# Weight sums made by DMA inside a two-layer encoder: regrouped in pairs, and started at other points

## What is computed

```python
def finish_layer(x, a, b, ga, gb, w_a, w_b, w_o, g1, b1, w_up, w_down, g2, b2):
    mix = (ga * (a @ w_a) + gb * (b @ w_b)) @ w_o
    x = layer_norm(ALPHA * x + mix, g1, b1)
    h = jnp.square(jax.nn.relu(x @ w_up)) @ w_down
    return layer_norm(ALPHA * x + h, g2, b2)
```

## Time and profile before

| what | value |
|---|---|
| three runs, median | 2154.99 us (2145.44 to 2157.51) |
| the profiled execution | 2145.24 us |
| its span, first to last instruction | 2143.4 us |
| PE busy | 2118.8 us, 99% of the span |
| DVE, ACT, POOL busy | 1471.3, 1230.3, 65.1 us |
| bytes moved by DMA | 399.27 MB, 186 GB/s in the mean |
| of them POOL's queue (q0) | 92.28 MB |

### The profile page before, as it was taken

One profiled execution on the slowest core, in us unless ns is written; L12 is line 12 of the kernel. 1 busy time (PEld: TensorE's weight loads), 2 busy tenths in 40 slices (PEclk: granted clock), 3 DMA queues, 4 the chain that ended last, 5 costly groups with the idle time before them and its releaser, 6 DMA issues.

```text
span 2143.4 us, 38213 instructions
## 1 busy us (share of the span) xinstructions
PE 2118.8 (99%) x15004; PEld 1936.0 (90%) x15004; DVE 1471.3 (69%) x2336; ACT 1230.3 (57%) x2493; POOL 65.1 (3%) x100
## 2 busy tenths in 40 slices
PE   9999999999989999999999999999999899999998
PEld 7998889999979898989889888899999798989897
DVE  6757777677869356665667577786768693566646
ACT  4457776696525356656234677766865253656561
POOL 1100000001000000000001000000010000000000
PEclk9999999999999999999999999999999999999999
DMA  7877562577894345454368765525778932454541
GB/s 256 240 279 258 210 234 82 159 238 213 222 323 104 103 130 172 151 166 139 108 189 245 289 249 202 205 88 177 223 203 255 294 105 93 139 171 152 168 148 69
DMA packets 100866, 399.27 MB, mean 186 GB/s; under 512 B 15272, under 2 KB 16936, under 8 KB 87600
## 3 DMA queue, kind: packets, MB, share of 16 engines
q1 hardware_dynamic: 67904, 191.55, 26.3%
q0 software_dynamic: 7936, 92.28, 17.2%
q10 hardware_dynamic: 24848, 112.99, 14.7%
HBM read 367.42 MB, written 118.23 MB: 227 GB/s over the span
## 4 chain that ended last, share of the span: by engine, by line
PE 96%; DMA 2%; ACT 1%; DVE 1%; issue 0%; SPq 0%; DVEq 0%; ACTq 0%
PE PS L826 9%; PE PS L828 9%; PE PS L827 9%; PE PS L1047 6%; PE PS L1049 6%; PE PS L1048 6%; PE PS L916 5%; PE PS L917 5%; PE PS L915 5%; PE PS L860 4%; PE PS L861 4%; PE PS L859 4%; PE PS L986 3%; PE PS L987 3%; PE PS L985 3%; PE PS L1175 2%
## 5 line engine op out<-in xcount | busy, mean ns | idle before, releaser
L826 PE MATMUL PS<-xt_hi,w_hi 128*128 128x320 f32 x1184 | 382.1, 323 | 0.3
L828 PE MATMUL PS<-xt_hi,w_lo 128*128 128x320 f32 x1184 | 365.7, 309 | 0.0
L827 PE MATMUL PS<-xt_lo,w_hi 128*128 128x320 f32 x1184 | 365.5, 309 | 0.0
L2539 DVE TENSOR_TENSOR w_lo<-w_raw,w_hi 128x1024 fp32r<-128x1024 f32 x146 | 177.3, 1222 | 162.0 <-ACT w_hi L1577 160.4
L2546 DVE TENSOR_TENSOR w_lo<-w_raw,w_hi 128x1024 fp32r<-128x1024 f32 (+1 forms) x176 | 199.2, 1138 | 114.9 <-ACT w_hi L1593 114.6
L1577 ACT ACTIVATE w_hi<-w_raw 128x1024 fp32r<-128x1024 f32 x146 | 153.3, 1059 | 189.6 <-PE PS L1049 155.8
L826 PEld LDWEIGHTS PS<-xt_hi,w_hi 128*128 128x128 f32 x1184 | 222.7, 188 | 5.4 <-issue 4.3
L827 PEld LDWEIGHTS PS<-xt_lo,w_hi 128*128 128x128 f32 x1184 | 223.0, 188 | 0.1
L828 PEld LDWEIGHTS PS<-xt_hi,w_lo 128*128 128x128 f32 x1184 | 222.2, 188 | 0.0
L1593 ACT ACTIVATE w_hi<-w_raw 128x1024 fp32r<-128x1024 f32 (+1 forms) x176 | 172.2, 984 | 86.1 <-PE PS L987 66.3
L1047 PE MATMUL PS<-w_hi,act_a_hi 128*128 128x512 f32 x480 | 189.7, 395 | 13.2 <-DVE rows L3005 13.2
(11 more groups left out here) (391 smaller groups left out, 5088.2 us busy)
## 6 DMA issues: line engine op xcount, KB each, us to landing
w_raw<-in_weights SPq DMA_DIRECT2D x186, 512.0 KB, 4.6
kc<-in_k_cache ACTq DMA_DIRECT2D x32, 1024.0 KB, 7.5
vc<-in_v_cache ACTq DMA_DIRECT2D x16, 2048.0 KB, 8.7
w_raw<-up_sums SPq DMA_DIRECT2D x112, 256.0 KB, 2.8
up_sums<-in_up_blocks POOLq DMA_DIRECT2D x24, 1024.0 KB, 10.1
w_raw<-in_up_blocks SPq DMA_DIRECT2D x84, 256.0 KB, 2.8
down_sums<-in_down_blocks POOLq DMA_DIRECT2D x16, 1024.0 KB, 10.6
w_raw<-in_down_blocks SPq DMA_DIRECT2D x32, 512.0 KB, 3.5
```

Source lines behind the costliest of these rows:

```text
L826: mm(out, wh, hi[:, k, c], start=(k == 0), stop=False)
L827: mm(out, wh, lo[:, k, c], start=False, stop=False)
L828: last = mm(out, wl, hi[:, k, c], start=False, stop=(k == KT - 1))
L2539: v.tensor_tensor(w_lo[slot][:], raw[:, raw_of(s, n)[0], :], w_hi[slot][:].bitcast(F32), ALU.subtract)\
```

## The change

The six jobs of a layer stay, with the same sources, destinations and bytes. Three things are different. First, a function `sums_of` takes a list of jobs and issues each step for all of them before it waits: with two jobs a step has four or two transfers outstanding where it had two or one. Second, the jobs run as (up 0, up 1) together, (down 1, up 2) together, down 2, up 3. Third, the starting points: (down 1, up 2) waits for the last product with the cached values of the layer (`dec_pv`), down 2 follows at once, and up 3 waits until the first weights of the plain down stage of part 0 are prepared. SP's waits follow: `JOBS_DONE` says how many jobs must be through before it fetches a job's sums (2, 2, 4, 4, 5, 6).

```diff
--- before.py
+++ after.py
@@ -159,8 +159,8 @@
 
 def sum_jobs():
 
-    return [(l, kind, part) for l in range(DEPTH) for part in range(FF_PARTS) for kind in ("up", "down")
-            if kind == "up" or part in BLOCK_PARTS]
+    order = (("up", 0), ("up", 1), ("down", 1), ("up", 2), ("down", 2), ("up", 3))
+    return [(l, kind, part) for l in range(DEPTH) for kind, part in order]
 
 
 SUM_JOBS = sum_jobs()
@@ -719,6 +719,7 @@
                         dst, src = raw[:, j, :], (down_blocks if kind[0] == "a" else down_sums)[l, b[0], b[1], p]
                     sp.dma_start(dst, src).then_inc(raw_loaded[j], 16)
 
+            JOBS_DONE = [6 * l + done for l in range(DEPTH) for done in (2, 2, 4, 4, 5, 6)]
             sums_at = {ring_pair(l, part, first_pair(part)): SUM_JOBS.index((l, "up", part))
                        for l in range(DEPTH) for part in range(FF_PARTS)}
             sums_at.update({ring_block(l, part): SUM_JOBS.index((l, "down", part))
@@ -735,7 +736,7 @@
                     sp.dma_start(raw[:, j, :], weights[n]).then_inc(raw_loaded[j], 16)
                 else:
                     if n in sums_at:
-                        sp.wait_ge(sum_dma, 16 * JOB_TRANSFERS * (sums_at[n] + 1))
+                        sp.wait_ge(sum_dma, 16 * JOB_TRANSFERS * JOBS_DONE[sums_at[n]])
                     load_ring(n, j)
                 if i == 36:
                     sp.dma_start(swk_keep_out, swa_k_keep).then_inc(keep_stored, 16)
@@ -761,51 +762,57 @@
             def add(dst, src):
                 pool.dma_start(dst, src, accum_op=ALU.add, max_dma_last_dim=8 * D).then_inc(sum_dma, 16)
 
-            def up_sums_of(l, part, before):
-
-                us = slice(UP_ORDER.index((part, first_pair(part))), UP_ORDER.index((part, FF_PAIRS - 1)) + 1)
-                a11, a12, a21, a22 = [flat_rows(up_blocks[l, b, us]) for b in range(4)]
-                s1, s2, s3, s4 = [flat_rows(up_sums[l, b, us]) for b in range(4)]
-                put(s1, a21)
-                put(s3, a11)
-                pool.wait_ge(sum_dma, 16 * (before + 2))
-                add(s1, a22)
-                add(s3, a21)
-                pool.wait_ge(sum_dma, 16 * (before + 4))
-                put(s2, s1)
-                pool.wait_ge(sum_dma, 16 * (before + 5))
-                add(s2, a11)
-                pool.wait_ge(sum_dma, 16 * (before + 6))
-                put(s4, s2)
-                pool.wait_ge(sum_dma, 16 * (before + 7))
-                add(s4, a12)
-                pool.wait_ge(sum_dma, 16 * (before + 8))
-
-            def down_sums_of(l, part, before):
-
-                b11, b12, b21, b22 = [flat_rows(down_blocks[l, part - 1, b]) for b in range(4)]
-                t1, t2, t3, t4 = [flat_rows(down_sums[l, part - 1, b]) for b in range(4)]
-                put(t1, b11)
-                put(t3, b22)
-                pool.wait_ge(sum_dma, 16 * (before + 2))
-                add(t1, b12)
-                add(t3, b12)
-                pool.wait_ge(sum_dma, 16 * (before + 4))
-                put(t2, t1)
-                pool.wait_ge(sum_dma, 16 * (before + 5))
-                add(t2, b22)
-                pool.wait_ge(sum_dma, 16 * (before + 6))
-                put(t4, t2)
-                pool.wait_ge(sum_dma, 16 * (before + 7))
-                add(t4, b21)
-                pool.wait_ge(sum_dma, 16 * (before + 8))
-
-            for j, (l, kind, part) in enumerate(SUM_JOBS):
-                if (kind, part) == ("up", 0):
-                    pool.wait_ge(w_ready[0], nth(l, AT_V) + 1)
-                elif (kind, part) == ("down", 1):
-                    pool.wait_ge(w_ready[0], nth(l, AT_SWA, 2) + 1)
-                (up_sums_of if kind == "up" else down_sums_of)(l, part, JOB_TRANSFERS * j)
+            def operands(l, kind, part):
+
+                if kind == "up":
+                    first, end = UP_ORDER.index((part, first_pair(part))), UP_ORDER.index((part, FF_PAIRS - 1)) + 1
+                    a, t = ([flat_rows(x[l, b, first:end]) for b in range(4)] for x in (up_blocks, up_sums))
+                    a11, a12, a21, a22 = a
+                    return t, (a21, a22, a11, a12, a11, a21)
+                a, t = ([flat_rows(x[l, part - 1, b]) for b in range(4)] for x in (down_blocks, down_sums))
+                b11, b12, b21, b22 = a
+                return t, (b11, b12, b22, b21, b22, b12)
+
+            def sums_of(jobs, before):
+
+                done = [before]
+
+                def all_done(transfers):
+                    done[0] += transfers * len(jobs)
+                    pool.wait_ge(sum_dma, 16 * done[0])
+
+                for (_, _, s3, _), (_, _, _, _, x3, _) in jobs:
+                    put(s3, x3)
+                for (s1, _, _, _), (x1, _, _, _, _, _) in jobs:
+                    put(s1, x1)
+                all_done(2)
+                for (s1, _, s3, _), (_, y1, _, _, _, y3) in jobs:
+                    add(s1, y1)
+                    add(s3, y3)
+                all_done(2)
+                for (s1, s2, _, _), _ in jobs:
+                    put(s2, s1)
+                all_done(1)
+                for (_, s2, _, _), (_, _, y2, _, _, _) in jobs:
+                    add(s2, y2)
+                all_done(1)
+                for (_, s2, _, s4), _ in jobs:
+                    put(s4, s2)
+                all_done(1)
+                for (_, _, _, s4), (_, _, _, y4, _, _) in jobs:
+                    add(s4, y4)
+                all_done(1)
+
+            for l in range(DEPTH):
+                before = JOB_TRANSFERS * SUM_JOBS.index((l, "up", 0))
+                pool.wait_ge(w_ready[0], nth(l, AT_V) + 1)
+                sums_of([operands(l, "up", 0), operands(l, "up", 1)], before)
+                pool.wait_ge(dec_pv, 2 * HEADS * (l + 1))
+                sums_of([operands(l, "down", 1), operands(l, "up", 2)], before + 2 * JOB_TRANSFERS)
+                sums_of([operands(l, "down", 2)], before + 4 * JOB_TRANSFERS)
+                pool.wait_ge(w_ready[0], down_at(l, 0) + 1)
+                sums_of([operands(l, "up", 3)], before + 5 * JOB_TRANSFERS)
+
 
         @block.tensor
         def _(pe):
```

## The result

Median of four runs 2190.2 us (2181.7 to 2198.7), of before 2154.5 us in the same four rounds; the ratio is 1.0187, with a 95% interval from 1.0160 to 1.0215; the two medians alone give 1.0166, inside it. All ratios compare fast executions: one of the kernel before at 2325.6 us and one of experiment 12 at 5403.5 us stand apart and are left out. The profiled execution took 2198.7 us, with a span of 2196.9; against the 2143.4 of before that is 53.5 us more.

A forecast was written before the change was run, and what follows sets the result against it. PE was taken to bound the kernel, busy 2118.8 of 2143.4 us. 2145.2 − 15.6 (w_o waits and clock) + 20 (branch a) = 2149.6 us, 2159 beside the median, 0.2% more; range 2134 to 2182.

The forecast's parts named there:

- what bounds the kernel, and the gain: PE busy 2118.8 of 2143.4 us; removing two waits and their slow clock was to gain 15.6 us.
- The w_o waits: Two PE waits for DVE's taking of w_o results, one a layer, 13.2 us together; both were to go.
- the clock: PE's slow clock after a stop, 1.2 us a time: twice saved at w_o, three times paid in branch a.
- the timing of POOL's group: Down 1 with up 2 from 336 to some 441 us, then down 2 alone to about 497.
- (a): Start of the layer, up 0 with up 1 side by side: taken at 0.
- (b): Plain down stage, up 3 running at 711 to about 767 us: taken at 0.
- (c): Window attention, with down 2 there instead of down 1 and up 2: taken at 0.
- the gates' term of (d): Late gate fetches in branch a: six stops of 2.5 us, 15 us, and 2 us for the first pair.
- (d): Branch a, 373 to 423 us, both layers: two jobs beside it cost about 20 us, bounds 0 and 40.
- The bound of 5.4 us: In branch a, a gate fetch taking over 5.4 us stops PE, by the excess.
- the prediction's other reading: A fetch has to see POOL's whole step out; (d) would then be over 50 us.
- no gate finds a gap: Rival: all gates in branch a late, +40 instead of +20, 2179 us, 1.1% slower; chance 0.27.

The follow-up runs named there:

- experiment 12: Changed kernel with the group waiting for the early gates' stores, the first sigmoid behind the third seed, values' load and branch a's store behind the first swaps; 1.0065 of before.
- experiment 3: Kernel before with only up 3 moved, to wait for the plain down stage; 0.9921 of before.
- experiment 1: Changed kernel with down 1 and up 2, still side by side, at their old starting point in window attention; 0.9901 of before, 2127.1 us.
- Experiment 4: Kernel before with only up 0 and up 1 side by side at the start of the layer; 0.9988 of before.
- experiment 2: Changed kernel with its new starting points, but every job alone, one after the other; 1.0036 of before.
- experiment 6: Changed kernel with down 1 and up 2 also waiting until the four early gates are stored, about 365 us; 1.0075 of before.
- experiment 9: Kernel of experiment 8 with the window cache's values loaded ahead of its keys; 1.0011 of before.
- experiment 10: Kernel of experiment 8 with the cached values' load and the store of branch a behind ACT's first two swaps of window attention; 0.9989 of before.
- experiment 11: Kernel of experiment 8 with down 1 and up 2 one after the other; 0.9944 of before.
- experiment 5: Changed kernel with ACT's sigmoid of a pair's first gate in branch a moved behind the third seed copy; 1.0135 of before.
- experiment 7: Changed kernel with both the edit of experiment 5 and that of experiment 6; 1.0081 of before.
- experiment 8: Changed kernel with down 1 and up 2 waiting until branch a's last gate fetch has landed, about 421 us; 1.0024 of before.

## Why the prediction was wrong, step by step

It said 2159 us, 0.2% more, with a range to 2182; 2190 is outside. It missed by 31 us by the medians, by 1.7% in the ratio. Between the profiled executions it is more: 53.5 us were added where 4.4 were forecast (2149.6 − 2145.2), 49 us.

**Right: what bounds the kernel, and the gain.** The w_o waits come from up 3 in POOL's queue at 610 us: experiment 3 alone brings 0.79%, 17 us, where 15.6 were forecast. Within it the clock was put too low: 1.2 us was read off the first slow stretch, of 3 us, and the second lasts 6 (14 matmuls from 1692.5 to 1698.5, PEclk 0.50). PE's busy time is 3.4 us less without the two (2115.4 in experiment 1), not 2.4.

**Right: the timing of POOL's group.** 335.9 to 434.2 us (forecast 336 to 441), down 2 to some 499 (497), with 28 us for the four adds as forecast.

**Right: (a) and (b) at nothing.** Experiment 4 for (a), the full windows of plain down for (b). **Right only in part: (c) at nothing.** Once window attention is under way PE runs full beside POOL's jobs (experiment 1, 159.93 of 160 us), but at its start the changed kernel loses 11.7 us; more below.

**Mis-sized: the gates' term of (d).** Forecast 15 us for six stops and 2 for the first pair. Measured 23.6 in six stops and 2.0 with the first pair: the place and the number of stops were right, the mean wait was 3.9 us instead of 2.5. The bound of 5.4 us priced a late first gate about right or too high: at five stops a first gate was over it by 4.0, 4.0, 5.1, 6.1 and 5.4 us, and PE waited 3.98, 3.25, 3.30, 5.80 and 3.10. The sixth, 4.20 us at 1526.8, hangs on a pair's second gate, which took 12.2 us where the prediction gave it about 7 and no price. The fetches of the second to fourth pair took 6.0 to 12.2 us (first gates 9.4, 9.4, 10.5 and 11.5, 6.0, 10.8), the 2.5 was read off one job in branch b. For one job it was good: experiment 2 has 15.3. With two jobs side by side few fetches fell into a gap.

By the Trainium skill's rule on turn-taking between queues ("DMA: Bandwidth & Descriptors", "Queues, rings and completion order"), as the prediction read it, four transfers of POOL's cost a small one no more than two. The gates of the last three pairs met two at most and can't tell, but the stores can. In the median those of 320 KB took 2.9 and 2.2 us (`rope_c`, `rope_s`) with none outstanding, 7.4 and 3.9 beside one job, 12.3 and 12.9 beside two: the measurement decides, and here a small transfer does wait longer behind four than behind two. The DMA share rises with the number (0.26 before, 0.84 in experiment 2, 0.98 in the changed kernel, from 336 to 373 us), so that the two are not told apart. Nor does a small transfer always see POOL's step out, the prediction's other reading: the store of 340.60 landed 1 us behind the end of the four puts, those of 356.50 and 360.64 landed 12 and 5 us before the end of the four adds.

**The step that failed: (d), "Branch a, 373 to 423 us", was costed by its gate fetches alone, and (c), window attention, was put at nothing.** The group it was to meet lasts from 336 to 441 by the prediction's own sum, and nothing between 336 and 373 or behind 423 was looked at on ACT's queue. Two more sets of transfers stand on PE's path there. The early gates' stores, issued at 340 to 361 us, in the steps of four puts and four adds, must land before ACT may write `rope_s`: 12.0 us, shown by experiment 6. And the window cache's loads at the end of branch a, where ACT can't go on until they are handed over: 11.7 us. That a long issue makes the swap late is shown by experiments 9 to 12; in the changed kernel the issue lasts 8.3 and 9.0 us beside down 2's two adds. This belongs to (c) as much as to (d): the earlier trace rows, on which (c) rests, begin at 435, when these loads (423.1 and 423.8 before) are through, and by the prediction's own times they were to meet the group's last steps. I had read the timeline of ACT only at its second pair. These 23.7 us, with four of the ten slow stretches at some 2 us each, are about 32 of the 49 us; the rest is the gates' 8.6 (25.6 instead of 17) and the clock behind them.

**Mis-sized with them: the clock.** Forecast 1.2 us a stop for three of six stops. PE's busy time grew by 18.0 us although two slow stretches went (3.4 us by experiment 1): 21.4 us over ten falls, 2.1 us each. Both were too small, and the number more than the size: the prediction counted stops of over 4 us only, and the clock fell at stops of 3.1 to 3.3 us too.

**The rivals.** The nearest was the third, "no gate finds a gap", 2179 us at 0.27, with the right place and too small a bound, since it too held gates alone.

What stays open: how much of the 1.9% each wait is worth by itself. The repairs of experiments 5 to 7 and 12 move ACT against POOL's steps, and each changes the others' waits, so that prices taken from them don't add up.

## What to carry to other kernels

When a background transfer is moved, list every transfer of every other queue in its new stretch, stores as well as loads, and for each ask who waits for it to land and which engine issues it; then ask the same of one step further, where its end falls. A stretch where PE is full and the DMA share is 0.47 can still be the worst place for it, and one with 0.83, window attention once its cache is loaded, a good one (experiment 1): what counts is who hangs on a small transfer with how many us in hand. And split such a change before it is judged: here one added wait (experiment 3) brings 0.8%, and the rest of the change costs 2.7% on top of it (1.0187 / 0.9921).

## What was not expected of the hardware

- A DMA instruction right behind a load of 2048 rows of 256 bytes lasts about as long as POOL's step has left: 12.4 to 13.2 us near the start of a step of four puts (experiments 8 and 9), 3.2 to 10.0 in steps of two, 1.6 and 1.9 near the end of a step of one, and 1.4 to 1.6 with none outstanding. Nothing that stands behind it in ACT's order starts meanwhile. The profile calls it "issue" at the next instruction. POOL has idle times of the same name, as 9.57 us ahead of the second of two adds, at 426.24 in the changed kernel; no run here shows what it stood for.
- Small transfers pay for large ones beside them, and more for four than for two: a store of 320 KB went from 2.2 to 12.9 us.
